# Five merged pairs a layer in place of four in a split-precision feed-forward, and the weight sums of the next pair issued earlier on VectorE

## The chip, the cores and the metric

The kernel runs on one core of one Trainium2 chip. The metric is the device time of one execution in microseconds (us), as the median of several executions. Five engines work in parallel, each through its own list of instructions, and they meet only at semaphores: TensorE (PE in the profile: matmuls and, as PEld, the loads of their stationary operand), VectorE (DVE), ScalarE (ACT), GpSimd (POOL) and SyncE (SP), which here only issues the loads of weights.

## The reference: what is computed

The program is a chain of blocks over 256 tokens of 1024 features in float32: two layers of (feed-forward, mixer, feed-forward, gated addition) and a third block with three kinds of attention and an MLP. The change touches only the feed-forward, which occurs four times:

```python
def swiglu(x, w_gu, w_down):
    g, u = jnp.split(x @ w_gu, 2, axis=-1)
    return (jax.nn.silu(g) * u) @ w_down
...
h = h + 0.5 * swiglu(rmsnorm(h, ffn1_norm[i]), ffn1_w_gu[i], ffn1_w_down[i])
```

`w_gu` is 1024 x 5632 and `w_down` 2816 x 1024. The product with `w_down` has 22 blocks of 128 rows (k), two halves of the tokens (t) and two halves of 512 output columns (c).

## The kernel before

**Split products.** A float32 product is made of three matmuls in a reduced format. Every operand is split into a high part and the rest: ScalarE copies a weight tile `raw` to `whi` (line 1547), VectorE subtracts `whi` from `raw` into `wlo` (line 2130), and TensorE computes x_hi·w_hi + x_hi·w_lo + x_lo·w_hi (line 626). Weight tiles have up to 2048 elements per partition. They go through 4 buffers `raw` and through 3 buffers `whi`/`wlo` (`NSPL`), so the split of tile n must wait until TensorE has finished tile n-3. `take(...)` of a tile on ScalarE and VectorE calls `ahead`, which emits the splits up to two tiles further on.

**Merged pairs.** In the product with `w_down`, blocks k = 2j and 2j+1 can be treated as a 2 x 2 block product (two token halves, two k blocks, two column halves) with seven block products in place of eight. `PAIRS` says for how many j this is done; the other k blocks take the classic eight. Such a pair needs differences of activations (GpSimd, `differences`, and their splits, `high_d` and `low_d`) and sums of weights (VectorE, `sums`: one addition of 1024 columns and two of 512 into a buffer `ts0`, `ts1` or `ts2`). Its weights form two tiles. "paired" j holds the loaded weights, of which 1536 columns are split; TensorE uses it in 9 matmuls. "mixed" j is the 2048 columns of sums; TensorE uses it in 12 matmuls. A classic tile ("down", called rest in the code) of 4 k blocks takes 24 matmuls of 512 columns, one of 2 k blocks 12.

**The order of tiles** is fixed by `down_tiles`. With four pairs it is: rest, pair 0, rest, pair 1, rest, pair 2, rest, pair 3, short rest (2 k blocks), and then the three closing tiles (4, 4 and 2 k blocks). Here I write R0, P0, M0, R1, P1, M1, R2, P2, M2, R3, P3, M3, R4, L0, L1, L2, with P for paired and M for mixed. M_j cannot be split before `sums` of pair j, and `sums` of pair j cannot start before the raw weights of P_j have landed. After L0, VectorE folds the merged accumulators into the residual (`merged`) while TensorE works on L0.

**Ahead of the first pair** TensorE also transposes the last activation block (`turn_a(10)`, after R0). It is evacuated from bank 4 by ScalarE (`high_a(10)`) and VectorE (`low_a(10)`), and the first matmul of M0 writes to bank 4, so it waits for `low_a(10)` (`clear(4)`).

Of the kernel before, what the change touches and what calls it, by code (L numbers as in the profile page):

```python
# [17 lines left out]
TOP = 3e38  # L18
NRAW, NSPL = 4, 3
TILE = 2048  # L20
PAIRS = 4


C_ID, C_HALF = 0, 128
# [58 lines left out]
class Events:  # L83
# [8 lines left out]
    def sig(self, name, *key, by=1):  # L92
        sem = SEMAPHORE.get(name, name)
        self.count[sem] = self.count.get(sem, 0) + by
        self.noted[(name,) + key] = self.count[sem]
        return self.sems[sem], by

    def at(self, name, *key):
        return SEMAPHORE.get(name, name), self.known[(name,) + key] if self.known else 0
# [36 lines left out]
def f(x):  # L136
    return x.bitcast(F32)


def flat(x):  # L140
    return x.rearrange("p a b -> p (a b)")
# [101 lines left out]
def down_tiles(pairs):  # L243

    tiles, middle, last = {}, ([], []), [(0, 18, 22), (1, 16, 20), (1, 20, 22)]
    for c, end in ((0, 18), (1, 16)):
        for k in range(2 * pairs, end, 4):
            middle[c].append((c, len(middle[c])))
            tiles[middle[c][-1]] = (k, min(4, end - k))
    closing = []  # L250
    for c, k, end in last:
        closing.append((c, sum(x[0] == c for x in tiles)))
        tiles[closing[-1]] = (k, end - k)
    others = [x for pair in itertools.zip_longest(middle[1], middle[0][1:]) for x in pair if x]
    order = [("rest", middle[0][0])]
    for j in range(pairs):
        order.append(("pair", j))
        if others:
            order.append(("rest", others.pop(0)))
    return order + [("rest", x) for x in others], tiles, closing  # L260


DOWN_ORDER, DOWN_TILES, DOWN_LAST = down_tiles(PAIRS)
HALVES = 2 * len(PREP) + 2
# [108 lines left out]
def pair(c):  # L373
    return (0, 1) if c % 2 == 0 else (2, 3)
# [19 lines left out]
def programs(dr, mem, banks, plan, ev):  # L394
# [9 lines left out]
    tile = plan.index  # L404
# [7 lines left out]
    labels = list(plan.index)  # L412

    def columns_of_tile(n):

        _, a, b = plan.tiles[n]
        return slice(512 if labels[n][0] == "paired" else 0, a * b)

    def wsplit(name, n):
        return mem[name][:, n % NSPL, columns_of_tile(n)]  # L420

    def wsource(n):

        if labels[n][0] == "mixed":
            return mem[f"ts{labels[n][2] % 3}"][:, :]
        return mem["raw"][:, plan.raw_of[n] % NRAW, columns_of_tile(n)]

    def landed(n):

        if labels[n][0] == "mixed":  # L430
            return at("tsum", *labels[n][1:])
        return at(f"d_w{plan.raw_of[n] % NRAW}", n)
# [4 lines left out]
    def rstd(r, t):  # L437
        return st[:, 33 + 2 * (r % 2) + t:34 + 2 * (r % 2) + t]
# [33 lines left out]
    def bank_half(b, j):  # L472
        return banks[b][:, j * 256:j * 256 + 256]
# [79 lines left out]
    def sync(S):  # L553
# [25 lines left out]
        def table():  # L579
            rp = dr["rpb"]  # L580
            S.wait_ge(*at("w_rel", "mixed", 2, PAIRS - 1))
            for y in range(2):
# [39 lines left out]
    def tensor(T):  # L622
# [13 lines left out]
        def take(*label):  # L636
            n = T.n
            T.n += 1
            if tile[label] != n:
                raise ValueError(label)  # L640
            T.wait_ge(*at("w_hi", n))
            T.wait_ge(*at("w_lo", n))
            return wview("whi", n), wview("wlo", n)
# [182 lines left out]
        def mixed_down(i, r, turn_last):  # L826
# [29 lines left out]
            def seven(j):  # L856
                first, final = j == 0, j == PAIRS - 1
                hi, lo = take("paired", i, j)
                T.wait_ge(*at("aTlo", i, j))
                T.wait_ge(*at("dTlo", i, j))  # L860
                three_products(0, block_of(2 * j, 0), hi[:, 0, 512:1024], lo[:, 0, 512:1024], first, final)
                three_products(2, difference(j, 2), hi[:, 1, 0:512], lo[:, 1, 0:512], first, False)
                three_products(6, block_of(2 * j + 1, 0), hi[:, 1, 512:1024], lo[:, 1, 512:1024], False, False).then_inc(
                    *sig("w_rel", "paired", i, j))
                hi, lo = take("mixed", i, j)
                if first:
                    clear(4)
                three_products(4, difference(j, 0), hi[:, 0, :], lo[:, 0, :], first, final)
                three_products(5, block_of(2 * j, 1), hi[:, 1, :], lo[:, 1, :], first, final)
                three_products(1, difference(j, 1), hi[:, 2, :], lo[:, 2, :], first, final)  # L870
                three_products(7, block_of(2 * j + 1, 1), hi[:, 3, :], lo[:, 3, :], False, False).then_inc(*sig("w_rel", "mixed", i, j))
# [668 lines left out]
    def scalar(A):  # L1540
        e = A.e

        def act(out, in_, func, **kw):
            return e.activation(out, in_, func, **kw)  # L1544

        def copy(out, in_, **kw):
            return e.activation(out, in_, ACT.Identity, **kw)  # L1547
# [13 lines left out]
        def take(*label, hold=0):  # L1561
            n = A.n
            A.n += 1
            if tile[label] != n:
                raise ValueError(label)
            ahead(n + NSPL - hold)
# [45 lines left out]
        def ffn(i, r, extra=None):  # L1612
            fa, aThi = mem["fa"], mem["aThi"]

            def high_a(c):
                A.wait_ge(*at("turn_a", i, c))
                b = banks[4 + c % 2]
                if c >= PAIRS:
                    copy(flat(aThi[:, 2 * c:2 * c + 2, :]), b).then_inc(*sig("aThi", i, c))
# [7 lines left out]
            def high_d(c):  # L1627

                A.wait_ge(*at("dsum", i, c))
                d = mem["dsum"][:, c % 2, :]  # L1630
                copy(aThi[:, 2 * c, P:256], d[:, 0:P])
                copy(flat(mem["dThi"][:, c, :, :]), d[:, P:512]).then_inc(*sig("dThi", i, c))

            def mixed_down(r):
                take("down", i, 0, 0)
                high_a(10)
                for what, x in DOWN_ORDER[1:]:
# [4 lines left out]
                    take("mixed", i, x)  # L1642
                A.wait_ge(*at("w_rel", "paired", i, PAIRS - 1))
                copy(flat(mem["ftmp"][:, :, :]), banks[0], scale=0.5).then_inc(*sig("root", i))
# [14 lines left out]
            for c in range(11):  # L1659
# [9 lines left out]
                for t in range(2):  # L1669
# [4 lines left out]
                    act(mem["ftmp"][:, t, :], bank_half(pair(c)[t], 0), ACT.Silu, scale=rstd(r, t)).then_inc(*sig("ftmp", i, c, t))  # L1674
                if 1 <= c <= PAIRS:
                    high_d(c - 1)
# [449 lines left out]
    def vector(V):  # L2126
        e = V.e

        def tt(out, a, b, op):
            return e.tensor_tensor(out, a, b, op)  # L2130
# [4 lines left out]
        def sums(n):  # L2135

            i, j = labels[n][1:]
            w, o = mem["raw"][:, plan.raw_of[n] % NRAW, :], mem[f"ts{j % 3}"][:, :]
            halves = lambda x: x.rearrange("p (x c) -> p x c", x=2)
            V.wait_ge(*landed(n))  # L2140
            if j >= 3:
                V.wait_ge(*at("w_lo", tile["mixed", i, j - 3]))
            elif j:
                V.wait_ge(*at("w_rel", "up", i, 10, 1))
            else:
                V.wait_ge(*at("dTlo", i, PAIRS - 1))
            tt(halves(o[:, 0:1024]), halves(w[:, 512:1536]), w[:, 0:512].unsqueeze(1).to_broadcast([P, 2, 512]), ALU.add).then_inc(*sig("tfirst", i, j))
            V.wait_ge(*at("tfirst", i, j))
            tt(o[:, 1024:1536], o[:, 0:512], w[:, 1024:1536], ALU.add).then_inc(*sig("tsecond", i, j))
            V.wait_ge(*at("tsecond", i, j))  # L2150
            tt(o[:, 1536:2048], o[:, 1024:1536], w[:, 1536:2048], ALU.add).then_inc(*sig("tsum", i, j))

        def ahead(m):
            while V.ready < min(m, len(plan.tiles)):
                n = V.ready
                V.ready += 1
                if labels[n][0] == "paired":
                    sums(n)
                V.wait_ge(*at("w_hi", n))
                tt(wsplit("wlo", n), wsource(n), f(wsplit("whi", n)), ALU.subtract).then_inc(*sig("w_lo", n))  # L2160

        split4 = lambda x: x.rearrange("p (a b) -> p a b", a=4)

        def take(*label, hold=0):
            n = V.n
            V.n += 1
            if tile[label] != n:
                raise ValueError(label)
            ahead(n + NSPL - hold)
# [594 lines left out]
        low(0, 1, 1)  # L2764
        begin(1, (0, 1, 2, 3))
        ahead(3)
        mean_square(0, 0)
        mean_square(0, 1)
# [17 lines left out]
    def gpsimd(G):  # L2786
# [114 lines left out]
        rstds(10)  # L2901

    return dict(S=sync, T=tensor, A=scalar, V=vector, G=gpsimd)


# [155 lines left out]
```

## Time and profile before

| what | value |
|---|---|
| median of 3 executions | 1668.43 us (1668.39 to 1669.02) |
| time of the profiled execution | 1669.16 us |
| its span, first to last instruction | 1667.4 us |
| mean granted TensorE clock | 0.998 |
| busy: PE, PEld, DVE, ACT, POOL | 1655.6, 1416.9, 1164.0, 941.0, 121.1 us |

Matmuls are pipelined and their ends are modelled: one of 512 columns is shown with 0.39 us, but the next starts earlier. The time that one costs is read from start to start, and a TensorE wait of less than about 0.2 us is not shown as idle at all. Rows of a timeline give start, duration, engine, line, operation, output and inputs, the number merged into the row, and in brackets the idle time before it with what ended it.

### The profile page before, as it was taken

To read this page: it belongs to the slowest core of one execution; us is meant where nothing else is said; L and a number is where in the kernel's file an instruction comes from. 1 tells how busy PE (TensorE), PEld (TensorE's weight loads), DVE (VectorE), ACT (ScalarE), POOL (GpSimd) and SP (SyncE) were. 2 spreads that over 40 slices of the span, in tenths; PEclk is the share of its full clock that TensorE was granted. 3 is DMA by queue.
4 is the path that set the end of the run, shared out by engine and by line. 5 is a ranking of instruction groups with operands and counts; after the bars stand their busy time and mean duration, and the time that the engine had idled before them with its cause. 6 is when DMAs were issued, how large, how long until landed. Compare 5 with 4: busy or idle time off the path is not lost.

```text
span 1667.4 us, 23289 instructions
## 1 busy us (share of the span) xinstructions
PE 1655.6 (99%) x9318; PEld 1416.9 (85%) x9318; DVE 1164.0 (70%) x1500; ACT 941.0 (56%) x1363; POOL 121.1 (7%) x135
## 2 busy tenths in 40 slices
PE   9999999999999999999999999999999999999998
PEld 7888899999788888888887778888889999988886
DVE  5657878999966568755688767567855578776643
ACT  6545567777865445754456666545653556564532
POOL 1000000000111000010006401000000000000000
PEclk9999999999999999999999999999999999999999
DMA  9655677666566646666486336654655533465551
GB/s 308 195 177 164 193 184 210 180 190 212 156 194 198 195 156 207 194 184 195 154 233 234 116 112 205 191 184 164 218 182 165 161 102 127 157 210 177 177 194 58
DMA packets 244235, 300.58 MB, mean 180 GB/s; under 512 B 9505, under 2 KB 175777, under 8 KB 244129
## 3 DMA queue, kind: packets, MB, share of 16 engines
q1 hardware_dynamic: 238624, 289.52, 55.1%
q10 hardware_dynamic: 5504, 9.58, 2.2%
q8 instruction: 74, 1.21, 0.3%
q14 instruction: 33, 0.26, 0.0%
HBM read 297.96 MB, written 1.11 MB: 179 GB/s over the span
## 4 chain that ended last, share of the span: by engine, by line
PE 96%; DVE 2%; POOL 1%; ACT 0%; DMA 0%; issue 0%; DVEq 0%; ACTq 0%
PE bank L626 93%; PE bank L629 4%; DVE wlo L2130 1%; POOL bm L2790 0%; POOL st L2790 0%; DMA prm<-in_prm 0%; DVE hTlo L2133 0%; ACT hThi L1547 0%; DVE rTlo L2133 0%; DVE xn L2133 0%; DVE h L2133 0%; ACT whi L1547 0%; ACT rThi L1547 0%; DVE xn L2200 0%; DVE qn L2133 0%
## 5 line engine op out<-in xcount | busy, mean ns | idle before, releaser
L2130 DVE TENSOR_TENSOR wlo<-raw,whi 128x2048 fp32r<-128x2048 f32 (+2 forms) x284 | 616.5, 2176 | 232.0 <-ACT whi L1547 232.0
L1547 ACT ACTIVATE whi<-raw 128x2048 fp32r<-128x2048 f32 (+2 forms) x284 | 511.9, 1809 | 167.5 <-PE bank L626 162.6
L626 PE MATMUL bank<-whi,hThi 128*128 128x512 f32 x1056 | 420.6, 398 | 0.4 <-DVE wlo L2130 0.4
L626 PE MATMUL bank<-wlo,hThi 128*128 128x512 f32 x1056 | 412.6, 391 | 0.8 <-DVE wlo L2130 0.8
L626 PE MATMUL bank<-whi,hTlo 128*128 128x512 f32 x1056 | 397.0, 391 | 0.0
L626 PE MATMUL bank<-hThi,whi 128*128 128x256 f32 x888 | 253.4, 285 | 0.0
L626 PE MATMUL bank<-hThi,wlo 128*128 128x256 f32 x888 | 251.2, 283 | 0.0
L626 PE MATMUL bank<-hTlo,whi 128*128 128x256 f32 x888 | 251.2, 283 | 0.0
L626 PEld LDWEIGHTS bank<-whi,hThi 128*128 128x128 f32 x1056 | 198.8, 188 | 44.9 <-issue 6.5
L626 PEld LDWEIGHTS bank<-whi,hTlo 128*128 128x128 f32 x1056 | 198.5, 188 | 42.6 <-DVE hTlo L2133 0.2
L626 PEld LDWEIGHTS bank<-wlo,hThi 128*128 128x128 f32 x1056 | 198.9, 188 | 40.4 <-DVE wlo L2130 1.7
L626 PEld LDWEIGHTS bank<-hThi,whi 128*128 128x128 f32 x888 | 169.5, 191 | 3.7 <-issue 3.1
L626 PEld LDWEIGHTS bank<-hThi,wlo 128*128 128x128 f32 x888 | 169.5, 191 | 0.2
L626 PEld LDWEIGHTS bank<-hTlo,whi 128*128 128x128 f32 x888 | 169.5, 191 | 0.2
L626 PE MATMUL bank<-whi,aThi 128*128 128x512 f32 x288 | 113.6, 395 | 0.5
L626 PE MATMUL bank<-whi,aTlo 128*128 128x512 f32 x288 | 112.3, 390 | 0.0
L626 PE MATMUL bank<-wlo,aThi 128*128 128x512 f32 x288 | 112.1, 389 | 0.0
L1544 ACT ACTIVATE ftmp<-bank,st 128x256 f32<-128x256 f32 x88 | 41.5, 474 | 101.5 <-PE bank L626 101.5
L2130 DVE TENSOR_TENSOR aTlo<-bank,aThi 128x512 fp32r<-128x512 f32 (+2 forms) x60 | 29.4, 512 | 77.9 <-ACT aThi L1547 77.9
L1547 ACT ACTIVATE aThi<-bank 128x512 fp32r<-128x512 f32 (+2 forms) x60 | 25.5, 456 | 98.3 <-PE bank L629 98.3
L2790 POOL TENSOR_TENSOR st<-st,cst 128x1 f32<-128x1 f32 (+2 forms) x35 | 36.9, 1070 | 457.3 <-DVE st L2173 433.1
L1547 ACT ACTIVATE hThi<-bank,prm 128x128 fp32r<-128x128 f32 (+1 forms) x152 | 43.5, 380 | 46.3 <-PE bank L629 42.7
(245 smaller groups left out, 2153.2 us busy)
## 6 DMA issues: line engine op xcount, KB each, us to landing
raw<-in_ffn_w_gu SPq DMA_DIRECT2D x172, 512.0 KB, 4.9
raw<-in_w_in SPq DMA_DIRECT2D x30, 1024.0 KB, 5.3
raw<-in_ffn_w_down SPq DMA_DIRECT2D x24, 1024.0 KB, 5.0
raw<-in_ffn_w_down SPq DMA_DIRECT2D x40, 512.0 KB, 4.0
raw<-in_ssd_w_in SPq DMA_DIRECT2D x16, 1024.0 KB, 5.8
raw<-in_ssd_w_in SPq DMA_DIRECT2D x32, 512.0 KB, 5.8
raw<-in_w_up SPq DMA_DIRECT2D x16, 1024.0 KB, 5.4
raw<-in_w_down SPq DMA_DIRECT2D x16, 1024.0 KB, 5.0
```

Source lines behind the costliest of these rows:

```text
L626: return T.e.matmul(out, lhsT, rhs, start=start, stop=stop, skip_group_check=skip)
L629: return T.e.transpose(out, in_, ident)
L1544: return e.activation(out, in_, func, **kw)
L1547: return e.activation(out, in_, ACT.Identity, **kw)
L2130: return e.tensor_tensor(out, a, b, op)
L2790: return e.tensor_tensor(out, a, b, op)
```

## The change

Two edits. `PAIRS` becomes 5, so that k blocks 8 and 9 are treated as pair 4. And on VectorE the sums of pair j+1 are no longer emitted directly ahead of the split of P_(j+1), but directly behind the split of M_j; the sums of pair 0 stay where they were.

```diff
-PAIRS = 4
+PAIRS = 5
...
-                if labels[n][0] == "paired":
+                if labels[n][0] == "paired" and labels[n][2] == 0:
                     sums(n)
                 V.wait_ge(*at("w_hi", n))
                 tt(wsplit("wlo", n), wsource(n), f(wsplit("whi", n)), ALU.subtract).then_inc(*sig("w_lo", n))
+                if labels[n][0] == "mixed" and labels[n][2] + 1 < PAIRS:
+                    sums(tile["paired", labels[n][1], labels[n][2] + 1])
```

`down_tiles(5)` gives another order of tiles as well: R0, P0, M0, R1, P1, M1, R2, P2, M2, R3, P3, M3, P4, M4, L0, L1, L2. R3 now has 2 k blocks instead of 4, R4 is gone, and P4 follows M3 directly.

VectorE at the start of the product with `w_down`; `ts_74`, `ts_75` and `ts_76` are the buffers `ts0`, `ts1`, `ts2`, `aTlo<-bank` is `low_a(10)`, the first row is the split of M0, the split of 2048 from `raw` is that of R1 and the one of 1536 that of P1:

```order
 L2130 TENSOR_TENSOR wlo<-ts_74,whi 128x2048
-L2130 TENSOR_TENSOR aTlo<-bank,aThi 128x512
-L2130 TENSOR_TENSOR wlo<-raw,whi 128x2048
 L2130 TENSOR_TENSOR ts_75<-raw 128x1024
 L2130 TENSOR_TENSOR ts_75<-ts_75,raw 128x512 x2
+L2130 TENSOR_TENSOR aTlo<-bank,aThi 128x512
+L2130 TENSOR_TENSOR wlo<-raw,whi 128x2048
 L2130 TENSOR_TENSOR wlo<-raw,whi 128x1536
```

The sums of pair 1 have moved ahead of `low_a(10)` and of the split of R1.

VectorE at the end of that product, from the sums of pair 3 to the closing tiles:

```order
 L2130 TENSOR_TENSOR ts_74<-raw 128x1024
 L2130 TENSOR_TENSOR ts_74<-ts_74,raw 128x512 x2
+L2130 TENSOR_TENSOR wlo<-raw,whi 128x1024
 L2130 TENSOR_TENSOR wlo<-raw,whi 128x1536
 L2130 TENSOR_TENSOR wlo<-ts_74,whi 128x2048
-L2130 TENSOR_TENSOR wlo<-raw,whi 128x1024
+L2130 TENSOR_TENSOR ts_75<-raw 128x1024
+L2130 TENSOR_TENSOR ts_75<-ts_75,raw 128x512 x2
+L2130 TENSOR_TENSOR wlo<-raw,whi 128x1536
+L2130 TENSOR_TENSOR wlo<-ts_75,whi 128x2048
 L2130 TENSOR_TENSOR wlo<-raw,whi 128x2048 x2
 L2130 TENSOR_TENSOR wlo<-raw,whi 128x1024
```

The split of the short R4 behind M3 has given way to the sums of pair 4 and the splits of P4 and M4; the short rest (the first added row, R3) now stands ahead of P3.

## Rows read from the trace of the kernel before

**Rows 1.** The page: busy time by engine, and the granted clock in 40 slices.
```profile
PE 1655.6 (99%) x9318; PEld 1416.9 (85%) x9318; DVE 1164.0 (70%) x1500; ACT 941.0 (56%) x1363; POOL 121.1 (7%) x135
...
PEclk9999999999999999999999999999999999999999
```
**Rows 2.** The page: the chain that ended last, by line.
```profile
PE bank L626 93%; PE bank L629 4%; DVE wlo L2130 1%; POOL bm L2790 0%; POOL st L2790 0%; DMA prm<-in_prm 0%; DVE hTlo L2133 0%; ACT hThi L1547 0%; DVE rTlo L2133 0%; DVE xn L2133 0%; DVE h L2133 0%; ACT whi L1547 0%; ACT rThi L1547 0%; DVE xn L2200 0%; DVE qn L2133 0%
```
**Rows 3.** Timeline of PE: P0, M0, start of R1; last, R1 in the second feed-forward.
```profile
141.74 0.48 PE L626 MATMUL bank<-whi,aThi 128*128 128x512 f32 x1
...
143.89 0.39 PE L626 MATMUL bank<-whi,dThi 128*128 128x512 f32 x1
...
146.39 0.39 PE L626 MATMUL bank<-whi,aTlo 128*128 128x512 f32 x1
146.89 0.47 PE L626 MATMUL bank<-whi,aThi 128*128 128x512 f32 x1
147.20 0.39 PE L626 MATMUL bank<-wlo,aThi 128*128 128x512 f32 x1
...
612.56 0.39 PE L626 MATMUL bank<-whi,aTlo 128*128 128x512 f32 x1
613.06 0.47 PE L626 MATMUL bank<-whi,aThi 128*128 128x512 f32 x1
```
**Rows 4.** Timeline of PE: first matmuls of R2, P3, M3 and L0.
```profile
157.22 0.40 PE L626 MATMUL bank<-whi,aThi 128*128 128x512 f32 x1
...
172.89 0.39 PE L626 MATMUL bank<-whi,aThi 128*128 128x512 f32 x1
...
174.93 0.39 PE L626 MATMUL bank<-whi,dThi 128*128 128x512 f32 x1
...
180.37 0.39 PE L626 MATMUL bank<-whi,aThi 128*128 128x512 f32 x1
```
**Rows 5.** Timeline of DVE, same feed-forward: M0, low_a(10), R1, R2; then R3 to M3, merged.
```profile
138.45 2.29 DVE L2130 TENSOR_TENSOR wlo<-ts,whi 128x2048 fp32r<-128x2048 f32 x1 [1.32 <-ACT whi L1547]
142.65 0.69 DVE L2130 TENSOR_TENSOR aTlo<-bank,aThi 128x512 fp32r<-128x512 f32 x1 [1.90 <-ACT aThi L1547]
144.45 2.29 DVE L2130 TENSOR_TENSOR wlo<-raw,whi 128x2048 fp32r<-128x2048 f32 x1 [1.11 <-ACT whi L1547]
...
154.66 2.29 DVE L2130 TENSOR_TENSOR wlo<-raw,whi 128x2048 fp32r<-128x2048 f32 x1 [1.05 <-ACT whi L1547]
...
164.88 2.29 DVE L2130 TENSOR_TENSOR wlo<-raw,whi 128x2048 fp32r<-128x2048 f32 x1 [1.06 <-ACT whi L1547]
167.08 1.22 DVE L2130 TENSOR_TENSOR ts<-raw 128x1024 f32<-128x1024 f32 x1
...
169.68 1.75 DVE L2130 TENSOR_TENSOR wlo<-raw,whi 128x1536 fp32r<-128x1536 f32 x1
171.75 2.29 DVE L2130 TENSOR_TENSOR wlo<-ts,whi 128x2048 fp32r<-128x2048 f32 x1 [0.32 <-ACT whi L1547]
...
183.20 0.68 DVE L2133 SCALAR_TENSOR_TENSOR h<-bank,h 128x512 f32<-128x512 f32 x1
```
**Rows 6.** Timeline of ACT: R1 and P1 split; R3 and P3; M3; R4.
```profile
142.51 3.28 ACT L1547 ACTIVATE whi<-raw 128x2048 fp32r<-128x2048 f32 x2
...
162.93 3.53 ACT L1547 ACTIVATE whi<-raw 128x2048 fp32r<-128x2048 f32 x2 [1.43 <-PE bank L626]
169.79 1.92 ACT L1547 ACTIVATE whi<-ts 128x2048 fp32r<-128x2048 f32 x1 [3.33 <-DVE ts L2130]
173.15 1.06 ACT L1547 ACTIVATE whi<-raw 128x1024 fp32r<-128x1024 f32 x1 [1.43 <-PE bank L626]
```
**Rows 7.** Issues of weight loads (the page): queue, count, size, median us to landing.
```profile
raw<-in_ffn_w_down SPq DMA_DIRECT2D x40, 512.0 KB, 4.0
```
**Rows 8.** Timeline of DVE during the fourth activation block: split of the tile two ahead.
```profile
65.34 2.29 DVE L2130 TENSOR_TENSOR wlo<-raw,whi 128x2048 fp32r<-128x2048 f32 x1 [1.18 <-ACT whi L1547]
```
**Rows 9.** Timeline of PE: the transposes directly ahead of that tile.
```profile
73.20 0.60 PE L629 MATMUL bank<-cst,fa 128*128 128x128 f32 x4
```

## The prediction

> **What bounds the kernel now.** I read the page first: TensorE is busy for 99% of the span at the full granted clock [rows 1], and the chain that ended last is TensorE's matmuls to 97% [rows 2]. So two things only can change the time: the number of matmuls, and the moments at which TensorE waits. Neither shows in busy time, because the ends of matmuls are modelled. I therefore went to the timeline of TensorE and read starts. In the product with w_down nine matmuls of P0 run from 143.89 back to 141.74, and M3's 12 and R4's 12 from 174.93 to 180.37: 5.44 us / 24 = 0.227 us from start to start, not the 0.39 us that each shows [rows 3, 4]. A tile thus holds TensorE for 5.46 us (24 matmuls), 2.73 us (12) or 2.05 us (9). The one irregular step in that product is at R1: its first matmul starts 0.50 us after the last of M0 (0.27 us of waiting), and the next follows at 0.31 us, not 0.227, so each restart costs some 0.08 us more [rows 3]. VectorE's split of R1 ends at 144.45 + 2.29 = 146.74 [rows 5], so a matmul starts 0.15 us after the split that it waited for. The second feed-forward has the same step at the same place, 612.56 to 613.06 [rows 3], and the other two have it too, so one feed-forward stands for all four.
>
> **What is removed.** Three matmuls of 512 columns in each of four feed-forwards: 12 x 0.227 = **2.7 us**, 0.16% of the time. The row, not the shown duration, prices it: by 0.39 us each it would be 4.7 us. The Trainium skill ("TensorE: Matmul & The Clock Gate", Back-to-back issue gap) puts a sustained stream at about 131 ns for a matmul of 512 columns, and an isolated one at about 216 ns. By the first figure the saving would be an estimate of 1.6 us only, by the second 2.6 us; the trace has 227 ns, near the second, and decides.
>
> **What is added under cover.** A fifth set of activation differences: GpSimd has nothing else to do there, ScalarE copies some 0.4 us more and VectorE subtracts some 0.8 us more. The pattern is that of block c = 3 today: there the split of a tile is done at 65.34 + 2.29 = 67.63, and TensorE comes to it behind the transposes of 73.20 [rows 8, 9]. The cover is over 5 us, so I take nothing. Without it, it would cost 0.8 us a feed-forward. Weight bytes are unchanged, and the loads stay 12 per product; P4 goes into the buffer that R2's split frees at 154.66 + 2.29 = 156.95, needed at 171.9, against 4.0 us to landing for each of its halves [rows 5, 7]. SyncE issues in order, and nothing ahead of that load waits for later work.
>
> **What is moved, at the start.** Sums of pair 1 now follow the split of M0 (of 2048 columns; the next operation starts 167.08 - 164.88 = 2.20 us after its start, so at 138.45 + 2.20 = 140.65). The three additions take 169.68 - 167.08 = 2.60 us [rows 5], to 143.25. Behind them waits low_a(10), today at 142.65; it ends then at 143.25 + 0.69 = 143.94 and TensorE can begin M0 at 144.09, where it began at 143.89 [rows 3, 5]. M0 ends at 144.09 + 2.73 + 0.08 = 146.90, and R1, whose split does not move (ScalarE's copy starts at 142.51 and takes 1.9 us [rows 6], VectorE is free again at 143.9), was started at 146.89. The new wait takes the place of the old one: between 0 and 0.1 us gained, as one restart may vanish. In the middle rounds the earlier sums remove idle time of ScalarE (3.33 us ahead of each mixed split [rows 6]), but TensorE doesn't wait for that today, so it is worth nothing.
>
> **What is moved, at the end.** This is where I expect the loss. Up to R3 everything is as before. R3 has 12 matmuls fewer, so P3 starts at 172.89 - 2.73 = 170.16 [rows 4], M3 at 172.21, P4 at 174.94 if nothing waits, M4 at 176.99, L0 at 179.72.
>
> The three buffers whi/wlo tie a split to the tile three back. ScalarE starts 0.26 us after that tile's successor has begun (R4 takes the place of R3 and is copied at 173.15; P3, next after R3, started at 172.89 [rows 4, 6]). A copy of 2048 columns takes 1.92 us and a split 2.29 [rows 5, 6]. In order:
>
> M3 takes M2's place. R3 starts 5.46 us ahead of today's P3, at 167.43, so ScalarE copies M3 from 167.7 to 169.6, VectorE splits it to 171.95 and TensorE may start at 172.1: in time, with 0.1 us to spare. Today the sums hold the same copy back to 169.79 and it doesn't matter, since R3 is long.
>
> Sums of pair 4 come next on VectorE: from 171.86 to 174.46. They can't be earlier, as they stand behind the split of M3. Behind them the split of P4 takes 1.75 us [rows 5], to 176.2, and TensorE may start P4 at 176.36. That is **1.4 us late**.
>
> M4 is copied by ScalarE as soon as the sums are there, 174.5 to 176.45, split from 176.5 to 178.8, and may start at 178.9. P4 with its restart ends at 176.36 + 2.05 + 0.08 = 178.5: **0.4 us late** again. M4 with another restart ends at 178.92 + 2.73 + 0.08 = 181.73. L0 is copied behind M4, to 178.4, split to 181.1: in time. L1 and L2 follow in the rhythm of today, and merged begins 2.8 us after L0's start, as it did (183.20 against 180.37 [rows 4, 5]).
>
> So L0 starts at 181.73 where it started at 180.37: 1.36 us later. This is -0.68 for the three matmuls, +1.42 and +0.42 of waiting, +0.17 of restarts and rounding. Less 0 to 0.1 us at the start it is +1.3 us a feed-forward, four times: **+5.3 us**. From the profiled execution, 1667.4 us of span and 1669.16 us of time, that leads to 1672.7 and 1674.5; as that execution is 0.7 us above the median of 1668.43, I state 1668.4 + 5.3 = **1673.7 us**.
>
> The two waits are bounded so. From below: if pair 4's sums were fully hidden, 0. From above: P4's and M4's splits hang in one chain behind M3's, so if M3's comes later than I read by x (its 0.1 us to spare is less than my error may be), L0 starts later by x more: 1.9 us in place of 1.36 for x = 0.5, 2.3 us for x = 0.9, which is about what the idle time ahead of a split varies by in these rows (0.32 to 1.32 us [rows 5]).
>
> **The rivals.** *The wait is hidden and the saving remains* (not slower). For it: VectorE is idle for about a third of the kernel [rows 1], and the earlier sums give it slack in each middle round. Against it: this slack can't be carried over M3's split, since that waits for ScalarE, which waits for TensorE. It needs the work on VectorE between M3's split and P4 to be short by 1.4 us. Time then 1668.4 - 2.7 = 1665.7 us. The mechanism turns at a total wait of 0.68 us a feed-forward: below it the change gains, above it loses. Even then the gain is under 0.2%, which is about what a measurement of this kernel can tell from no change.
>
> *The waits are there but shorter*: if TensorE comes late to P4 for another reason, or the sums run faster where nothing shares the memory with them, by 0.6 us or more of the 1.9. Time 1668 to 1671.5 us, partly within 0.2%.
>
> *The loss is larger*: M3 late as well, or P1's weights not landed at 140.7, when the moved sums first ask for them. Against the second: its buffer is freed by the split of the last activation tile, three tiles ahead of M0, and a landing takes 4.0 us [rows 7]. Time 1675.5 to 1677.5 us (4 x 1.9 and 4 x 2.3 above 1668.4).
>
> *Gain over 0.2%*: it would need the saving of 2.7 us and all four waits at R1 (0.35 us each with the restart) together. R1's split doesn't move, so I see no way to it.
>
> **How the numbers follow.** Forecast (slower by 4 to 6.5 us) 0.65; larger loss 0.12; shorter waits 0.12, half of it within 0.2%; hidden 0.08, within 0.2%; over 0.2% faster 0.03. A change of 0.2% is 3.3 us. So slower 0.82, same 0.15, faster 0.03. The range of eight in ten runs from 1669.5 (waits of 0.95 us a feed-forward in place of 1.9) to 1677.0 us.
>
> **What would show it.** In the timeline of TensorE: a step of about 1.6 us from the last matmul of M3 to the first of P4, one of 0.6 us from P4 to M4, in each of four feed-forwards; M0 some 0.2 us late in place of R1; a total of 12 matmuls fewer. In that of VectorE: the additions of pair 4 directly behind the split of M3 and directly ahead of that of P4, with no idle time. In the view of waits, TensorE waiting for wlo at eight more places. I am wrong if P4 starts with VectorE idle ahead of its split, or if TensorE shows steps in the middle rounds, where R2's split is today in time by 0.1 us only (156.95 + 0.15 against 157.22 [rows 4, 5]) and nothing in the change should touch it.

## The result and the profile after

| | before | changed kernel |
|---|---|---|
| median of 7 executions | 1668.99 us (1668.37 to 1669.55) | 1674.14 us (1673.96 to 1674.67) |
| span of the profiled execution | 1667.4 us | 1672.7 us |
| ratio to before | | 1.0033 (95% interval 1.0023 to 1.0042) |

The change makes the kernel slower by 5.15 us; 5.3 us were forecast, 1673.7 us as a time. The page after, its busy times and its granted clock:

```profile
PE 1656.0 (99%) x9306; PEld 1414.3 (85%) x9306; DVE 1179.6 (71%) x1528; ACT 950.4 (57%) x1383; POOL 132.0 (8%) x147
...
PEclk9999999999999999999999999999999999999999
```

TensorE has its 12 matmuls fewer and is nevertheless shown 0.4 us more busy than in [rows 1]. Nothing can be read from that number: the ends of matmuls are modelled, and a matmul that starts behind a wait is shown longer (0.47 us in place of 0.39). PEld, which loads the stationary operands, fell by 2.6 us; 12 loads of 0.19 us would be 2.3 us, but the kernel before and the one below with the sums moved have the same loads and differ by 1.2 us there (1416.9 and 1415.7), so this number shows little either. The loss has to be looked for in starts.

The timeline of TensorE in the first feed-forward: the last matmul of P0 and the first of M0; the first of R1; the last of M3 and the first of P4; the last of P4 and the first of M4; the first of L0.

```profile
143.91 0.39 PE L626 MATMUL bank<-whi,aTlo 128*128 128x512 f32 x1
144.33 0.47 PE L626 MATMUL bank<-whi,dThi 128*128 128x512 f32 x1
...
147.16 0.44 PE L626 MATMUL bank<-whi,aThi 128*128 128x512 f32 x1
...
174.95 0.39 PE L626 MATMUL bank<-whi,aTlo 128*128 128x512 f32 x1
176.53 0.47 PE L626 MATMUL bank<-whi,aThi 128*128 128x512 f32 x1 [1.19 <-issue]
...
178.46 0.40 PE L626 MATMUL bank<-whi,aTlo 128*128 128x512 f32 x1
179.18 0.47 PE L626 MATMUL bank<-whi,dThi 128*128 128x512 f32 x1 [0.33 <-DVE wlo L2130]
...
182.02 0.39 PE L626 MATMUL bank<-whi,aThi 128*128 128x512 f32 x1
```

The reader is to see steps of 0.42, 1.58 and 0.72 us where 0.227 is the undisturbed one. This execution runs 0.24 us later than that of before from its first matmuls on (P0 starts at 141.98 in place of 141.74), so L0 comes 182.02 - 0.24 - 180.37 = 1.41 us later than in [rows 4]; 1.36 was reckoned. The step of 0.42 has no bracket at all, as little as the wait of 0.27 us at R1 in [rows 3]. The other brackets show less than the wait, since they count from the modelled end of the matmul before, and the long one is put down to "issue", that is, to nothing that the view can name. The timeline of VectorE names it: the sums of pair 3 and the splits of R3, P3 and M3, then the sums of pair 4 and the splits of P4 and M4.

```profile
161.87 1.22 DVE L2130 TENSOR_TENSOR ts<-raw 128x1024 f32<-128x1024 f32 x1
163.12 1.42 DVE L2130 TENSOR_TENSOR ts<-ts,raw 128x512 f32<-128x512 f32 x2
164.46 1.22 DVE L2130 TENSOR_TENSOR wlo<-raw,whi 128x1024 fp32r<-128x1024 f32 x1
166.73 1.76 DVE L2130 TENSOR_TENSOR wlo<-raw,whi 128x1536 fp32r<-128x1536 f32 x1 [1.05 <-ACT whi L1547]
169.88 2.29 DVE L2130 TENSOR_TENSOR wlo<-ts,whi 128x2048 fp32r<-128x2048 f32 x1 [1.39 <-ACT whi L1547]
172.09 1.22 DVE L2130 TENSOR_TENSOR ts<-raw 128x1024 f32<-128x1024 f32 x1
173.34 1.42 DVE L2130 TENSOR_TENSOR ts<-ts,raw 128x512 f32<-128x512 f32 x2
174.68 1.75 DVE L2130 TENSOR_TENSOR wlo<-raw,whi 128x1536 fp32r<-128x1536 f32 x1
176.74 2.29 DVE L2130 TENSOR_TENSOR wlo<-ts,whi 128x2048 fp32r<-128x2048 f32 x1 [0.31 <-ACT whi L1547]
```

There is no idle time on VectorE between 169.88 and the end of P4's split at 176.43, and P4 starts 0.10 us behind it. But ahead of the splits of P3 and M3 VectorE sat idle for 1.05 and 1.39 us, waiting for ScalarE's copies. That P4 did not wait for its own copy is in the timeline of ScalarE (P4 and M4):

```profile
170.65 1.49 ACT L1547 ACTIVATE whi<-raw 128x1536 fp32r<-128x1536 f32 x1 [0.80 <-PE bank L626]
174.79 1.91 ACT L1547 ACTIVATE whi<-ts 128x2048 fp32r<-128x2048 f32 x1 [2.65 <-DVE ts L2130]
```

The copy was ready at 172.14, more than 2.5 us before VectorE came to the tile. M4's copy did wait for the sums.

All four feed-forwards have the same steps (1.58 or 1.59 us ahead of P4, 0.71 or 0.72 ahead of M4). From the first matmul of P0 to the first of the closing transposes the first one takes 47.52 us in place of 46.14, and the four together 5.44 us more. That stretch is used again below.

### The profile page after: what moved, and what is told of

Its sections match the earlier page's. It is cut to its first block, busy times and chain, and to the rows that moved or that the text cites. A ratio compares the mean times of both kernels' runs of the same rounds, so it can differ in the third digit from the quotient of the medians.

```text
span 1672.7 us, 23345 instructions
## 1 busy us (share of the span) xinstructions
PE 1656.0 (99%) x9306; PEld 1414.3 (85%) x9306; DVE 1179.6 (71%) x1528; ACT 950.4 (57%) x1383; POOL 132.0 (8%) x147
## 3 DMA queue, kind: packets, MB, share of 16 engines
HBM read 297.96 MB, written 1.11 MB: 179 GB/s over the span
## 4 chain that ended last, share of the span: by engine, by line
PE 96%; DVE 2%; ACT 1%; issue 1%; DVEq 0%; ACTq 0%
PE bank L626 92%; PE bank L629 4%; ACT whi L1547 1%; DVE wlo L2130 1%; DVE ts L2130 1%; DVE hTlo L2133 0%; ACT hThi L1547 0%; DVE rTlo L2133 0%; DVE xn L2133 0%; DVE h L2133 0%; ACT rThi L1547 0%; DVE xn L2202 0%; DVEq L2990 0%; ACT xn L1544 0%; DVE fa L2760 0%
## 5 line engine op out<-in xcount | busy, mean ns | idle before, releaser
L2130 DVE TENSOR_TENSOR wlo<-raw,whi 128x2048 fp32r<-128x2048 f32 (+2 forms) x284 | 609.8, 2156 | 217.9 <-ACT whi L1547 217.8
L626 PE MATMUL bank<-whi,aThi 128*128 128x512 f32 x272 | 107.7, 396 | 4.8 <-issue 4.8
L626 PE MATMUL bank<-whi,aTlo 128*128 128x512 f32 x272 | 106.1, 390 | 0.0
L626 PE MATMUL bank<-wlo,aThi 128*128 128x512 f32 x272 | 106.0, 390 | 0.0
L2130 DVE TENSOR_TENSOR aTlo<-bank,aThi 128x128 fp32r<-128x128 f32 (+1 forms) x64 | 29.0, 479 | 69.9 <-ACT aThi L1547 69.9
L1547 ACT ACTIVATE aThi<-bank 128x128 fp32r<-128x128 f32 (+1 forms) x64 | 25.3, 431 | 83.9 <-PE bank L629 83.9
```

The lines of the kernel that those rows point to most:

```text
L626: return T.e.matmul(out, lhsT, rhs, start=start, stop=stop, skip_group_check=skip)
```

## The experiments

The theory is that of the prediction: the loss is the queue on VectorE (sums of pair 4, split of P4) behind the split of M3, and nothing else. The rivals: the moved sums cost; the whi/wlo buffers come free too late; the fifth pair costs by its work in the activation blocks. The first four kernels ran together, the next four together, the last alone, each group with its own executions of the kernel before.

| kernel | median, us | before beside it, us | difference, us | ratio, 95% interval |
|---|---|---|---|---|
| five pairs, sums as before | 1674.94 | 1668.57 | +6.4 | 1.0025 to 1.0051 |
| four pairs, sums moved | 1668.66 | 1668.57 | +0.1 | 0.9992 to 1.0010 |
| pair 4's sums behind R3 | 1666.84 | 1668.57 | -1.7 | 0.9982 to 1.0000 |
| the same, and transposes inside R0 | 1665.40 | 1668.57 | -3.2 | 0.9973 to 0.9991 |
| two additions more | 1689.73 | 1668.50 | +21.2 | 1.0113 to 1.0144 |
| three matmuls put back | 1668.67 | 1668.50 | +0.2 | 0.9992 to 1.0009 |
| as the fourth, h21 on GpSimd | 1664.73 | 1668.50 | -3.8 | 0.9969 to 0.9986 |
| before, transposes inside R0 | 1667.11 | 1668.50 | -1.4 | 0.9982 to 1.0000 |
| one addition more | 1682.53 | 1668.62 | +13.9 | 1.0067 to 1.0101 |

**The two halves of the change, each alone.** Five pairs with the sums where they were:

```diff
-PAIRS = 4
+PAIRS = 5
```

> Five pairs, with the sums left directly ahead of the split of their own paired tile, as before. My theory (the loss sits where P4 follows M3, and is the wait for pair 4's sums behind M3's split): M3 and P4 are neighbours here too, so VectorE's order there is the same; about 5.2 to 5.8 us above before (1674.2 to 1674.8 us), with the steps of about 1.6 and 0.7 us ahead of P4 and M4, and R1 late by 0.27 us again in place of M0. Rival (the moved sums are what costs, by the queue ahead of low_a(10) or by asking for weights that have not landed): 2.7 us below before.

And four pairs with the sums moved:

```diff
-                if labels[n][0] == "paired":
+                if labels[n][0] == "paired" and labels[n][2] == 0:
                     sums(n)
...
+                if labels[n][0] == "mixed" and labels[n][2] + 1 < PAIRS:
+                    sums(tile["paired", labels[n][1], labels[n][2] + 1])
```

> Four pairs, with the sums moved. My theory: 0, within 0.4 us of before; M0 late by 0.2 us in place of R1 by 0.27 us, nothing else. Rival (the move costs): 5 us or more above before.

The fifth pair alone brings the whole loss (+6.4 us), the move alone nothing (+0.1). In the timeline of TensorE with five pairs only, the last matmul of M3 and the first of P4:

```profile
174.90 0.39 PE L626 MATMUL bank<-whi,aTlo 128*128 128x512 f32 x1
176.50 0.47 PE L626 MATMUL bank<-whi,aThi 128*128 128x512 f32 x1 [1.21 <-issue]
```

The step is the same 1.60 us. This kernel is about 1.2 us slower than the changed one (6.4 against 5.15), which I had put at 0 to 0.6. In its timeline the four stretches from P0 to the closing transposes are 0.85 us longer together than in the changed kernel. 0.6 us of that is at M3, which came 0.07 us late there and had a restart, because pair 3's sums stood between the splits of R3 and P3 and held M3's copy back. The remaining 0.35 us of the 1.2 is no more than the 0.4 us by which the two medians of before differ (1668.99 and 1668.57). With the sums moved and four pairs, M0 takes over the wait of R1:

```profile
143.70 0.39 PE L626 MATMUL bank<-whi,aTlo 128*128 128x512 f32 x1
144.11 0.47 PE L626 MATMUL bank<-whi,dThi 128*128 128x512 f32 x1
```

**Where the sums of pair 4 stand.** The changed kernel with these sums behind the split of R3:

```diff
-                if labels[n][0] == "mixed" and labels[n][2] + 1 < PAIRS:
+                if labels[n][0] == "mixed" and labels[n][2] + 1 < PAIRS - 1:
                     sums(tile["paired", labels[n][1], labels[n][2] + 1])
+                if labels[n][0] == "down" and labels[n][2:] == (1, 1):
+                    sums(tile["paired", labels[n][1], PAIRS - 1])
```

> The changed kernel with one thing different: the sums of pair 4 stand behind the split of R3 and not behind that of M3. My theory: P4's split then starts as soon as ScalarE has copied it and is done some 1.3 us ahead of need, M4's some 0.2 us ahead; both waits vanish and the 12 matmuls remain saved: 2.7 us below before, 7.9 us below the changed kernel (about 1666.2 us). Rival 1 (P4 is late since its whi/wlo buffer comes free late): no difference to the changed kernel. Rival 2 (the fifth pair costs through its additional work in the activation blocks or its traffic): most of the 5.2 us remains.

The same instructions in another order on one engine, and 5.15 us of loss become 1.7 us of gain. The interval of the gain reaches 1.0000, but the timeline has it in each feed-forward: 45.62 us from P0 to the closing transposes where before took 46.14. Both rivals fall: buffers, loads and the work of the activation blocks are those of the changed kernel. VectorE in that kernel, from the sums of pair 4 on (then P3, M3, P4, M4):

```profile
165.58 1.22 DVE L2130 TENSOR_TENSOR ts<-raw 128x1024 f32<-128x1024 f32 x1
166.83 1.42 DVE L2130 TENSOR_TENSOR ts<-ts,raw 128x512 f32<-128x512 f32 x2
168.16 1.75 DVE L2130 TENSOR_TENSOR wlo<-raw,whi 128x1536 fp32r<-128x1536 f32 x1
169.87 2.29 DVE L2130 TENSOR_TENSOR wlo<-ts,whi 128x2048 fp32r<-128x2048 f32 x1
172.16 1.76 DVE L2130 TENSOR_TENSOR wlo<-raw,whi 128x1536 fp32r<-128x1536 f32 x1
174.63 2.29 DVE L2130 TENSOR_TENSOR wlo<-ts,whi 128x2048 fp32r<-128x2048 f32 x1 [0.71 <-ACT whi L1547]
```

The sums fill the idle time ahead of P3 and M3, M3's split starts at 169.87 as before (169.88), and P4's follows it. But I expected 2.7 us of gain, and 1.7 came. A part of what is missing is 11 us behind P4, at the closing transposes, in the timeline of TensorE:

```profile
187.22 0.39 PE L626 MATMUL bank<-whi,aTlo 128*128 128x512 f32 x1
187.59 0.30 PE L629 MATMUL bank<-cst,h 128*128 128x128 f32 x1
```

A step of 0.37 us in place of 0.23: these transposes read the residual that VectorE updates behind `merged`, and VectorE came to `merged` 2.98 us after the first matmul of L0 (182.92 against 179.94) where before it was 2.83 us. With the three matmuls gone, the next thing was late by 0.15 us here and 0.19 us in the second feed-forward, 0.6 us in all four. By the timeline the four stretches are 2.2 us shorter than before; the other 0.4 us between that and the medians' 1.7 is not located.

**The opening of the product.** On top of that, the last transposes are issued in the middle of R0, and pair 1's sums stand behind `low_a(10)` (the diff is against the changed kernel):

```diff
                 for k in range(nk):
+                    if between and k == 2:
+                        between()
                     for t in range(2):
...
-            rest(0, 0)
-            turn_last()
+            rest(0, 0, turn_last)
...
-                if labels[n][0] == "mixed" and labels[n][2] + 1 < PAIRS:
+                if labels[n][0] == "mixed" and 0 < labels[n][2] < PAIRS - 2:
                     sums(tile["paired", labels[n][1], labels[n][2] + 1])
+                if labels[n][0] == "down" and labels[n][2:] == (1, 1):
+                    sums(tile["paired", labels[n][1], PAIRS - 1])
...
                 low_a(10)
+                sums(tile["paired", i, 1])
```

> The kernel of the earlier sums, and at the start of the product the last transposes in the middle of R0 in place of behind it, with pair 1's sums behind low_a(10). My theory: low_a(10) is then done 2 us ahead of M0, and R1's copy on ScalarE starts at R0's end, since high_a(10) is already through; the waits ahead of M0 and R1 (0.19 + 0.05 us, and two restarts of 0.08) vanish, 0.3 us four times: 1.0 to 1.5 us below the kernel of the earlier sums, about 1665.0 us, 4 us below before. Rival (this wait only moves on, since R1's split is now behind pair 1's sums): no difference.

1.4 us less than the kernel it is built on, as expected; no step at M0 or R1 is left. The same transposes alone, in the kernel before (first part of that diff):

> The kernel before with nothing but the last transposes in the middle of R0 in place of behind it. My theory: R1's copy starts at R0's end, 0.8 us sooner, its split is done at 145.9 where TensorE comes at 146.6; the wait of 0.27 us and its restart vanish: 0.35 x 4 = 1.4 us below before. Rival (the wait ahead of R1 was VectorE's, not ScalarE's): no difference.

1.4 us below before, in an interval that reaches 1.0000; the timeline of TensorE has no step at R1 in any of the four feed-forwards. `high_a(10)` on ScalarE in the kernel before, and below it the copy of R1 (and P1) and the last matmul of M0 and the first of R1 in this one:

```profile
142.02 0.60 ACT L1547 ACTIVATE aThi<-bank 128x512 fp32r<-128x512 f32 x1 [3.60 <-PE bank L629]
...
142.40 3.54 ACT L1548 ACTIVATE whi<-raw 128x2048 fp32r<-128x2048 f32 x2 [2.23 <-PE bank L626]
...
146.68 0.40 PE L626 MATMUL bank<-whi,aTlo 128*128 128x512 f32 x1
146.91 0.40 PE L626 MATMUL bank<-whi,aThi 128*128 128x512 f32 x1
```

Before, R1 waited for VectorE's split, VectorE for ScalarE's copy (1.11 us idle [rows 5]), and the copy stood behind `high_a(10)`, which waited for the transposes: so the wait ended with VectorE's split, but its cause was ScalarE's queue. The remedy is tighter than I expected. This execution runs 0.3 us late, so the copy starts only 0.4 us sooner and not 0.8, since it now waits for the last matmuls of R0; its split is done at 146.64 (146.34 in the time of before, where I had put 145.9), 0.27 us ahead of R1.

**The closing wait.** In the kernel of the opening the step ahead of the closing transposes is still 0.35 us. One addition of `merged` goes to GpSimd, and VectorE waits for it only ahead of the second of the two residual updates that follow:

```diff
@@ merged, on VectorE
-                V.wait_ge(*at("wm", i))
-                tt(h[:, 1, chunk(0)], h[:, 1, chunk(0)], wm, ALU.subtract).then_inc(*sig("h21", i))
...
@@ mixed_down, on VectorE
-                V.wait_ge(*at("h21", i))
                 for t in range(2):
+                    if t:
+                        V.wait_ge(*at("h21", i))
...
@@ ffn, on GpSimd
+            G.wait_ge(*at("wm", i))
+            tt(h[:, 1, chunk(0)], h[:, 1, chunk(0)], flat(mem["fa"][:, :, :]), ALU.subtract).then_inc(*sig("h21", i))
             G.wait_ge(*at("h12p", i))
```

> The best kernel so far (sums of pair 4 behind R3, transposes in the middle of R0) with one addition of merged (h21, 0.8 us on VectorE) given to GpSimd. In both kernels with the earlier sums the closing transposes start 0.12 to 0.19 us late, behind the residual update that follows merged on VectorE. My theory: this small wait goes, 0.12 to 0.19 us four times: 0.5 to 0.8 us less than that kernel, about 1664.7 us. Rival (GpSimd takes 1.7 us for it and the second residual update, then the second transposes, come late): 0 to 2 us more.

0.6 us less again, by the differences to before of the two groups; so small a difference rests on the timeline more than on the medians. The step ahead of the transposes is regular (186.62 to 186.86), in all four feed-forwards:

```profile
186.62 0.39 PE L626 MATMUL bank<-whi,aTlo 128*128 128x512 f32 x1
186.86 0.60 PE L629 MATMUL bank<-cst,h 128*128 128x128 f32 x4
```

This is the fastest kernel of the study, 1664.73 us, 3.8 us below before and 9 us below the changed one.

**The price of three matmuls.** The kernel with pair 4's sums behind R3, and one block of M4 multiplied twice, so that one term of the result is counted double:

```diff
+                if j == PAIRS - 1:
+                    three_products(5, block_of(2 * j, 1), hi[:, 1, :], lo[:, 1, :], False, final)
```

> The kernel of the earlier sums (five pairs without the wait) with three matmuls of 512 columns put back in each feed-forward, by multiplying one block of M4 twice (so its result is not that of the reference). Price by starts: 12 x 0.227 = 2.7 us above the kernel of the earlier sums, less up to 0.6 us, since they give VectorE 0.68 us more ahead of the closing transposes, which were 0.15 us late there. Rival (a matmul costs its shown 0.39 us): 4.7 us more. Rival (131 ns): 1.6 us more.

1.9 us more than without them (+0.2 against -1.7), a little under the 2.1 to 2.7 expected. In its timeline P0 to the closing transposes takes 187.87 - 141.73 = 46.14 us, and 187.59 - 141.97 = 45.62 us without: 0.52 us for three matmuls, which is 0.68 less the closing wait of 0.15 us that they made vanish. The price of 0.227 us a matmul holds; 0.39 (4.7 us) is excluded. By the medians alone, 1.9 us would fit the rival of 1.6 us as well; the starts exclude it, since they lie 0.227 us apart where nothing is waited for.

**A longer queue.** Two more additions of 1024 columns ahead of pair 4's sums in the changed kernel:

```diff
+            for x in range(2 if j == PAIRS - 1 else 0):
+                tt(halves(o[:, 0:1024]), halves(w[:, 512:1536]), w[:, 0:512].unsqueeze(1).to_broadcast([P, 2, 512]), ALU.add).then_inc(*sig("textra", i, x))
+                V.wait_ge(*at("textra", i, x))
```

> The changed kernel with two more additions of 1024 columns ahead of pair 4's sums (the same sums once more, results unchanged): 2 x 1.25 = 2.5 us more between M3's split and P4's. My theory (this queue alone sets P4's start): the step ahead of P4 grows from 1.58 to 4.1 us in each feed-forward, M4 stays 0.7 us behind; 10 us above the changed kernel, about 1683.8 us here. Rival (VectorE is not what P4 waits for, or its delay is partly absorbed further on): less than 5 us.

The step grew as reckoned, from 1.58 to 4.12 us:

```profile
174.54 0.39 PE L626 MATMUL bank<-whi,aTlo 128*128 128x512 f32 x1
178.66 0.47 PE L626 MATMUL bank<-whi,aThi 128*128 128x512 f32 x1 [3.73 <-issue]
```

The time grew by 16 us and not by 10. (The profiled execution was the fastest of the four: 1686.85 us, 12.35 us above the changed kernel's profiled one, at a mean granted clock of 0.996. The other three took 1689.7 to 1690.6 us at 0.993, and no timeline shows them.) So there was something more than the queue, and one addition in place of two was to tell where it begins:

> The changed kernel with one more addition of 1024 columns ahead of pair 4's sums in place of two. With two, the step ahead of P4 was 4.1 us as reckoned, but the time rose by 16 us more than the changed kernel's instead of 10, and the granted clock fell to 0.83 to 0.90 behind that step in three of four feed-forwards. Theory: with a step of 2.8 us the clock stays at 1.00 and only the queue counts: 4 x 1.25 = 5.0 us above the changed kernel, 10.2 us above before, about 1678.8 us. Rival (the clock falls here too, or the delay is absorbed): clearly over 1680, or under 1677.

Here too: 13.9 us above before, 8.7 us above the changed kernel's 5.15 in place of 5.0. The rival came true: the clock falls here too. My theory of the queue is right for the step (2.85 us, 1.27 more than 1.58) and wrong for what follows a long one. The timeline of TensorE at P4 in the fourth feed-forward of this kernel shows why:

```profile
1169.16 0.39 PE L626 MATMUL bank<-whi,aTlo 128*128 128x512 f32 x1
1172.01 0.63 PE L626 MATMUL bank<-whi,aThi 128*128 128x512 f32 x1 [2.46 <-issue]
1172.44 0.63 PE L626 MATMUL bank<-wlo,aThi 128*128 128x512 f32 x1
1172.87 0.63 PE L626 MATMUL bank<-whi,aTlo 128*128 128x512 f32 x1
1173.29 0.63 PE L626 MATMUL bank<-whi,dThi 128*128 128x512 f32 x1
```

From start to start they now take 0.43 us. The stretches of 5 us around it, and below them the first feed-forward of the same kernel. The granted clock is the number behind the busy times of the five engines:

```profile
core 0: us, PE busy (x) PEld busy (x) DVE busy (x) ACT busy (x) POOL busy (x), PEclk, DMA share, GB/s
1165.00:1170.00 5.00, 4.55 (x20) 3.37 (x19) 4.90 (x5) 1.36 (x1) 0.00 (x0) 1.00 0.18 69
1170.00:1175.00 5.00, 2.99 (x8) 2.35 (x8) 4.69 (x4) 3.71 (x2) 0.00 (x0) 0.72 0.33 108
1175.00:1180.00 5.00, 5.00 (x22) 4.14 (x21) 3.77 (x2) 3.46 (x3) 0.00 (x0) 0.94 0.65 213
...
175.00:180.00 5.00, 2.54 (x10) 1.94 (x9) 4.66 (x5) 3.72 (x2) 0.00 (x0) 0.89 0.23 52
180.00:185.00 5.00, 5.00 (x19) 3.96 (x18) 4.53 (x3) 3.10 (x3) 0.00 (x0) 0.77 0.30 66
```

The second feed-forward, where the clock did not fall, gives the price. From P0 to the closing transposes it takes 48.74 us, 1.2 more than in the changed kernel; the other three take 49.70 to 49.80. So the queue costs 1.2 to 1.3 us in each of the four, and the clock another 1.0 us in each of three: 8.0 us together, which is what the span of this execution has more than the changed kernel's (1680.7 and 1672.7 us).

## Why the prediction was right

**The saving** (12 x 0.227 = 2.7 us) was right; the matmuls put back confirm the price by starts. The figure of 131 ns that the Trainium skill gives ("TensorE: Matmul & The Clock Gate", Back-to-back issue gap) for a sustained stream is not met in any run here: 227 ns in all of them at the full clock.

**The work under cover** cost nothing that can be seen: the kernels with the sums of pair 4 elsewhere have all of it and are faster than before.

**The number.** 5.3 us were forecast and 5.15 measured. Part of this closeness is luck, since the medians of before differ by more between two sets (1668.43 and 1668.99). The starts are the firmer support: 5.44 us in the four stretches of the product, where 4 x 1.36 was reckoned.

**The start.** M0 was to come at 144.09 and came at 144.33 - 0.24 = 144.09; R1 at 146.9, and came at 147.16 - 0.24 = 146.92. The new wait took the place of the old one, and the move alone was worth nothing.

**The end.** P4 was to be 1.4 us late: 176.36 reckoned, 176.53 - 0.24 = 176.29 measured. M4: 178.92 and 178.94. L0: 181.73 and 181.78. That M3 had 0.1 us to spare was right as well; it started without a step, at 172.43. That the middle rounds stay regular was right.

**What was off.** `merged` began 2.5 us after the first matmul of L0 (184.52 against 182.02) and not 2.8, since L0 itself had become late and VectorE was ahead; it helped nothing. In the view of waits I expected eight more waits for wlo; the four long ones appear as "issue" and only the shorter ones as wlo. The time of the larger loss, 4 x 1.9 us above 1668.4, is 1676.0 and not 1675.5. And these bounds counted queues only. They left out that a longer wait on TensorE can also cost clock, which the runs with more additions showed (8.0 us in place of 5 in the profiled execution with one). At the waits of this change the clock stayed at 1.00, so the number was not touched by it.

**The rival that did not come true** (the wait is hidden, 1665.7 us) was one move away. I had argued that VectorE's idle time could not be carried over M3's split, and that holds for the code as it was changed. With the sums two splits earlier it is carried over, and 1666.84 us was measured.

## What to carry to other kernels

Price an instruction of a pipelined engine from start to start in the timeline, then ask of each engine that feeds it whether it keeps pace over every short stretch and not on average: here VectorE was 71% busy, and a queue of 2.6 us at the one place where two dense tiles became neighbours turned a saving of 2.7 us into a loss of 5. Work that depends on nothing late (sums of weights, here, whose buffer had been free for the load since 157.1, 15 us before the sums began, while a load lands 4.0 us after its issue) belongs ahead of an instruction that waits, into its idle time, and not behind it. When a stretch of the bounding engine is shortened, look for what is late next by less than the shortening: the closing transposes took back 0.6 us of the 2.7 here.

## What the runs showed of the hardware

A wait of TensorE can cost more than its length. With steps of 1.58 and 0.72 us (the changed kernel) the granted clock stayed at 1.00 in the stretches of 5 us around them, in all four feed-forwards. With one step of 2.85 us, 2.46 us of it shown as idle, the clock fell behind it in three of four feed-forwards, to 0.72 to 0.89 in the first stretch of 5 us, and matmuls of 512 columns came every 0.43 us in place of 0.227, which is the step from 2.4 to 1.2 GHz; after 6 to 9 of them the full clock was back. With 4.1 us it fell in three of the four of the profiled execution as well, not in the first. From P0 to the closing transposes a feed-forward with a fall took 0.7 to 1.1 us longer than the one without, in these two kernels. The same wait in the second feed-forward of the kernel with one addition, 2.85 us too, left the clock at 1.00. What tells the three from the fourth stays open.

At the full clock, the first matmul behind such a wait, or behind a group of transposes, was followed by the next after 0.30 to 0.32 us in place of 0.227 (176.53 to 176.83 in the changed kernel), so each restart costs 0.08 us by itself.
